# FFN first products turned round: the activations stand still, 512 weight columns move, and the gated values are turned back by TensorE

## The reference

```python
def rms_norm(x, g):
    y = xf * lax.rsqrt(jnp.mean(xf * xf, axis=-1, keepdims=True) + EPS)
    return (y * g.astype(jnp.float32)).astype(x.dtype)

def swiglu(h, w_gu, w_down):          # w_gu: 1024 x 5632, w_down: 2816 x 1024
    gate, up = jnp.split(h @ w_gu, 2, axis=-1)
    return (jax.nn.silu(gate) * up) @ w_down

x = x + 0.5 * swiglu(rms_norm(x, norm_ffn1[i]), w_ffn1_gu[i], w_ffn1_down[i])
```

## Time and profile before

| what | us |
|---|---|
| three runs | 1745.28, 1748.50, 1748.54 (median 1748.5) |
| the profiled execution: own time | 1747.14 |
| its span in the trace | 1745.4 |
| TensorE busy | 1680.4 (96%) |
| VectorE busy | 1073.2 (61%) |
| ScalarE busy | 797.5 (46%) |
| GpSimd busy | 158.6 (9%) |

### The profile page before, as it was taken

The page is one execution under the profiler, slowest core; times in us unless marked ns, Lnnn a source line. Parts: engine busy times, 40 slices in busy tenths (PEclk is TensorE's granted clock), DMA queues, the critical chain, the costliest instruction groups (busy, mean ns, idle before and its releaser), DMA issues.

```text
span 1745.4 us, 29133 instructions
## 1 busy us (share of the span) xinstructions
PE 1680.4 (96%) x12214; PEld 1579.1 (90%) x12214; DVE 1073.2 (61%) x1043; ACT 797.5 (46%) x934; POOL 158.6 (9%) x121
## 2 busy tenths in 40 slices
PE   7999998899999999999999999888999999999998
PEld 7999986799999999999999998776899989888997
DVE  6555776376456765678464686665665567556563
ACT  5443458254335543456343553544544465444442
POOL 1000122010001100012000135111000001100000
PEclk9999999999999999999999999888999999999999
DMA  7545451155454545454544353203255535325551
GB/s 278 216 150 213 151 185 75 73 200 186 174 194 164 198 165 197 172 200 184 187 182 178 146 204 145 97 25 120 79 211 177 184 145 193 108 110 187 178 189 48
DMA packets 39631, 282.26 MB, mean 162 GB/s; under 512 B 4416, under 2 KB 4544, under 8 KB 5760
## 3 DMA queue, kind: packets, MB, share of 16 engines
q1 hardware_dynamic: 39168, 279.59, 43.2%
q0 software_dynamic: 384, 1.51, 0.2%
HBM read 280.04 MB, written 1.05 MB: 161 GB/s over the span
## 4 chain that ended last, share of the span: by engine, by line
PE 88%; DVE 5%; ACT 4%; DMA 1%; issue 1%; POOL 1%; POOLq 0%; DVEq 0%; SPq 0%; ACTq 0%
PE ps L318 27%; PE ps L321 27%; PE ps L322 27%; DVE w_lo L1352 1%; DMA raw<-weights 1%; ACT arena L1166 1%; ACT w_hi L988 1%; PE ps L640 1%; PE ps L419 1%; PE ps L684 1%; DMA arena<-nsa_tables 0%; POOL arena L2015 0%; DVE arena L1647 0%; ACT arena L1018 0%; DVE arena L1588 0%
## 5 line engine op out<-in xcount | busy, mean ns | idle before, releaser
L318 PE MATMUL ps<-hT_hi,w_hi 128*128 128x256 f32 x2392 | 682.9, 285 | 14.2 <-DVE hT_lo L1364 11.3
L1352 DVE TENSOR_TENSOR w_lo<-raw,w_hi 128x2048 fp32r<-128x2048 f32 x264 | 600.8, 2299 | 139.0 <-ACT w_hi L988 139.0
L321 PE MATMUL ps<-hT_lo,w_hi 128*128 128x256 f32 x2392 | 678.7, 284 | 0.0
L322 PE MATMUL ps<-hT_hi,w_lo 128*128 128x256 f32 x2392 | 678.7, 284 | 0.0
L988 ACT ACTIVATE w_hi<-raw 128x2048 fp32r<-128x2048 f32 x264 | 495.2, 1903 | 56.3 <-DMA raw<-weights 50.7
L318 PEld LDWEIGHTS ps<-hT_hi,w_hi 128*128 128x128 f32 x2392 | 460.9, 193 | 17.3 <-DVE w_lo L1352 11.3
L321 PEld LDWEIGHTS ps<-hT_lo,w_hi 128*128 128x128 f32 x2392 | 461.2, 193 | 1.9 <-issue 0.7
L322 PEld LDWEIGHTS ps<-hT_hi,w_lo 128*128 128x128 f32 x2392 | 460.8, 193 | 0.0
L321 PE MATMUL ps<-hid_lo,w_hi 128*128 128x256 f32 x744 | 211.3, 284 | 0.0
L318 PE MATMUL ps<-hid_hi,w_hi 128*128 128x256 f32 x744 | 210.6, 283 | 0.0
L322 PE MATMUL ps<-hid_hi,w_lo 128*128 128x256 f32 x744 | 208.3, 280 | 0.0
(11 more groups left out here) (260 smaller groups left out, 1749.7 us busy)
## 6 DMA issues: line engine op xcount, KB each, us to landing
raw<-weights SPq DMA_DIRECT2D x264, 1024.0 KB, 4.8
X<-x SPq DMA_DIRECT2D x2, 512.0 KB, 7.3
out<-X SPq DMA_DIRECT2D x4, 256.0 KB, 2.1
arena<-p POOLq DMA_DIRECT2D x2, 256.0 KB, 5.4
arena<-counts POOLq DMA_DIRECT2D x1, 512.0 KB, 5.3
arena<-nsa_tables POOLq DMA_DIRECT2D x1, 448.0 KB, 7.3
const<-constants SPq DMA_DIRECT2D x1, 427.0 KB, 9.9
cols<-parameters SPq DMA_DIRECT2D x1, 213.5 KB, 2.7
```

The costliest lines, as they stand in the source:

```text
L318: mm = nc.tensor.matmul(dst, a_hi, b_hi, start=start, stop=False, skip_group_check=True)
L321: nc.tensor.matmul(dst, a_hi, b_lo, start=False, stop=False, skip_group_check=True)
L322: return nc.tensor.matmul(dst, a_lo, b_hi, start=False, stop=stop, skip_group_check=True)
L1352: nc.vector.tensor_tensor(unit_cols(w_lo, u, 0, UNIT), raw[:, r * UNIT:(r + 1) * UNIT], f(unit_cols(w_hi, u, 0, UNIT)), ALU.subtract).then ...
```

## The change

In FFN stages alone, `up` becomes `up_rows`: a 128 x 128 tile of `hT` (128 tokens) is stationary, and 512 weight columns (256 gate, 256 up) move, 2 token tiles x 3 products x 8 chunks, 48 matmuls of 512 columns. A bank then holds 128 tokens on the partitions, with gate and up side by side. ScalarE takes the silu straight from PSUM with `rstd` as the scale of each partition, in two halves of 256 columns; VectorE multiplies up by `rstd` and by that silu in one instruction for each half. `spread` goes from FFN stages. The product now has tokens on the partitions, and `down` wants hidden values there, so TensorE turns it with 4 transposes of 128 x 128 (`turn`) into the bank that the gates have left; `hid_hi` and `hid_lo` read that bank.

`turn(0)` stands ahead of chunk 4 of `up_rows(1)`, `turn(j)` for j from 1 to 9 ahead of chunk 1 of `up_rows(j + 1)`, and `turn(10)` ahead of the last quarter of `down(9)`.

```diff
@@ TensorE
-            def down(u, h, first, last, t=None):
+            def down(u, h, first, last, t=None, mid={}):
...
                 for b in range(4):
+                    if b in mid:
+                        mid[b]()
...
+                def up_rows(us, b0, fresh, t, mid):
+
+                    for k in range(KC):
+                        if k in mid:
+                            mid[k]()
+                        u, a = us[k // 4], k % 4 * 512
+                        if k % 4 == 0:
+                            unit_ready(u, t)
+                        if fresh:
+                            pe.wait_ge(*hT_ready.due(me))
+                        for tok in range(TT):
+                            mm = three(bank(b0 + tok), lhs(hT_hi, k, tok), lhs(hT_lo, k, tok), unit_cols(w_hi, u, a, 512), unit_cols(w_lo, u, a, 512),
+                                       k == 0, k == KC - 1)
+                            if (k, tok) == (KC - 1, 0):
+                                mm.then_inc(gu_full.sem, 1)
+                        if k % 4 == 3:
+                            mm.then_inc(unit_used.sem, 1)
+
+                def turn(j, t=None):
+
+                    pe.wait_ge(*rows_ready.due(me, turn=t))
+                    for c in range(HC):
+                        for tok in range(TT):
+                            mm = nc.tensor.transpose(bank(2 * (j % 2), c * TOKENS + tok * P, P), at(ACT_AT + tok * 256 + c * P, P), ident)
+                    mm.then_inc(rows_turned.sem, 1)
+
...
-                one(1, u0 + 2, mid={2: lambda: spread(7)})
+                rstd_ready.due(me)
+                one(1, u0 + 2, mid={4: lambda: turn(0)})
...
-                        one(2 + b, u + 3 * b, t)
+                        one(2 + b, u + 3 * b, t, {1: lambda: turn(1 + b, t)})
...
-                one(FFN_BLOCKS - 1, u)
+                one(FFN_BLOCKS - 1, u, mid={1: lambda: turn(FFN_BLOCKS - 2)}, in_down={3: lambda: turn(FFN_BLOCKS - 1)})
@@ ScalarE
-                    act.wait_ge(*scaled.due(me, turn=t))
-                    nc.scalar.activation(sil[:, 0:512], sil[:, 0:512], ACT.Silu).then_inc(silu_done.sem, 1)
+                    act.wait_ge(*gu_full.due(me, turn=t))
+                    nc.scalar.activation(sil[:, 0:256], bank(b0, 0, 256), ACT.Silu, scale=rstd[:, 0:1]).then_inc(silu_done.sem, 1)
+                    act.wait_ge(unit_used.sem, u + 2 + more)
+                    nc.scalar.activation(sil[:, 256:512], bank(b0 + 1, 0, 256), ACT.Silu, scale=rstd[:, 1:2]).then_inc(silu_done.sem, 1)
...
-                    act.wait_ge(*hid_ready.due(me, turn=t))
-                    if j and not last:
-                        act.wait_ge(unit_used.sem, u + 3 + more)
-                    nc.scalar.activation(chunk(hid_hi, HC if last else 0, HC), at(ACT_AT, 512), ACT.Copy).then_inc(hid_hi_done.sem, 1)
+                    act.wait_ge(*rows_turned.due(me, turn=t))
+                    nc.scalar.activation(chunk(hid_hi, HC if last else 0, HC), bank(b0), ACT.Copy).then_inc(hid_hi_done.sem, 1)
@@ VectorE
-                    times_rstd(sil[:, 0:512], bank(b0)).then_inc(scaled.sem, 1)
-                    times_rstd(second, bank(b0 + 1)).then_inc(second_scaled.sem, 1)
-                    nc.vector.tensor_tensor(at(ACT_AT, 512), sil[:, 0:512], second, ALU.mult).then_inc(hid_ready.sem, 1)
+                    for tok in range(TT):
+                        dve.wait_ge(*silu_done.due(me, turn=t))
+                        ins = nc.vector.scalar_tensor_tensor(at(ACT_AT + tok * 256, 256), bank(b0 + tok, 256, 256), rstd[:, tok:tok + 1],
+                                                             sil[:, tok * 256:(tok + 1) * 256], ALU.mult, ALU.mult)
+                    ins.then_inc(rows_ready.sem, 1)
...
-                    nc.vector.tensor_tensor(chunk(hid_lo, h, HC), at(ACT_AT, 512), f(chunk(hid_hi, h, HC)), ALU.subtract).then_inc(hid_split.sem, 1)
+                    nc.vector.tensor_tensor(chunk(hid_lo, h, HC), bank(b0), f(chunk(hid_hi, h, HC)), ALU.subtract).then_inc(hid_split.sem, 1)
```

More of the change, by code:

```diff
@@ L248, in network_kernel @@
         gu_full, scaled, silu_done, second_scaled = S("gu_full"), S("scaled"), S("silu_done"), S("second_scaled")
+        rows_ready, rows_turned = S("rows_ready"), S("rows_turned")
         hid_ready, hid_hi_done, hid_split = S("hid_ready"), S("hid_hi_done"), S("hid_split")
@@ L473, in ffn @@
             def ffn(s, u0):
-                def one(j, u, t=None, mid={}):
-                    up([u, u + 1], 2 * (j % 2), 4, gu_full, j == 0, t, mid)
+                def up_rows(us, b0, fresh, t, mid):
[14 more added lines that the diff above has]
+                            mm.then_inc(unit_used.sem, 1)
@@ new lines, in turn, with one @@
+                def turn(j, t=None):
[4 more added lines that the diff above has]
+                    mm.then_inc(rows_turned.sem, 1)
+                def one(j, u, t=None, mid={}, in_down={}):
+                    up_rows([u, u + 1], 2 * (j % 2), j == 0, t, mid)
@@ L478, in one @@
                     if j:
-                        down(u + 2, 0, j == 1, False, t)
+                        down(u + 2, 0, j == 1, False, t, in_down)
                 one(0, u0, mid={6: lambda: sums(s)})
-                one(1, u0 + 2, mid={2: lambda: spread(7)})
+                rstd_ready.due(me)
+                one(1, u0 + 2, mid={4: lambda: turn(0)})
                 u = u0 + 5
                 with pe.Fori(0, 4) as i:
-                    t = Turn(i, {hid_split: 2}, 6)
+                    t = Turn(i, {hid_split: 2, rows_ready: 2}, 6)
@@ L957, in ple @@
                 pe.wait_ge(*p_ready.due(me))
-                pe.wait_ge(rstd_read.sem, norm_of[s] + 1 - sum(kind in ("stick", "pool") for kind, _ in stages[:s]))
+                pe.wait_ge(rstd_read.sem, norm_of[s] + 1 - sum(kind in ("stick", "pool", "ffn") for kind, _ in stages[:s]))
                 for m in range(KC):
@@ L1023, in ffn @@
             def ffn(s, u0):
+                act.wait_ge(rstd_ready.sem, norm_of[s] + 1)
                 def one(j, u, t=None):
                     more = t.i * t.units if t else 0
[L1028 to L1029 removed]
+                    b0 = 2 * (j % 2)
+                    act.wait_ge(*gu_full.due(me, turn=t))
+                    nc.scalar.activation(sil[:, 0:256], bank(b0, 0, 256), ACT.Silu, scale=rstd[:, 0:1]).then_inc(silu_done.sem, 1)
+                    act.wait_ge(unit_used.sem, u + 2 + more)
+                    nc.scalar.activation(sil[:, 256:512], bank(b0 + 1, 0, 256), ACT.Silu, scale=rstd[:, 1:2]).then_inc(silu_done.sem, 1)
                     last = j == FFN_BLOCKS - 1
@@ L1043, in ffn @@
                 with act.Fori(0, 4) as i:
-                    t = Turn(i, {scaled: 2, hid_ready: 2}, 6)
+                    t = Turn(i, {gu_full: 2, rows_turned: 2}, 6)
                     for b in range(2):
                         one(2 + b, u + 3 * b, t)
-                scaled.due(me, 2 * 3)
-                hid_ready.due(me, 2 * 3)
+                gu_full.due(me, 2 * 3)
+                rows_turned.due(me, 2 * 3)
                 split[me] += 3 * 6
@@ L1307, in ple @@
             def ple(s, u0):
+                gu_full.due(me, 2)
                 nc.scalar.preload_act_table(ACT.Sigmoid)
@@ L1422, in ffn @@
                 split_to(u0 + 5)
-                take_rstd(7)
+                dve.wait_ge(rstd_ready.sem, norm_of[s] + 1)
                 one(0, u0)
@@ L1426, in ffn @@
                 u = u0 + 5
-                each = {silu_done: 2, second_scaled: 2, hid_hi_done: 2, hid_split: 2, gu_full: 2}
+                each = {silu_done: 4, hid_hi_done: 2}
                 with dve.Fori(0, 4) as i:
@@ L1436, in ffn @@
                 one(FFN_BLOCKS - 1, u)
-                hid_split.due(me)
+                gu_full.due(me, FFN_BLOCKS)
+                hid_split.due(me, FFN_BLOCKS)
             def mlp(s, u0):
```

8 lines of the change are left out of this document (1 added, 7 removed).

## The result

The changed kernel takes 1755.03 us (median of 10 runs, 1751.28 to 1757.21), the kernel before 1745.43 us (10 runs, 1743.79 to 1748.99). The ratio is 1.0049, with a 95% interval of 1.0040 to 1.0058: slower by half a per cent. The profiled execution took 1752.62 us, its span is 1750.9 us.

What follows compares the result with a forecast made beforehand. TensorE's list and its waits at stage ends were taken as the bound: -10.0 on the list, +6.9 at stage starts, +7.7 at ends, +4.6 us in all, forecast 1753.0 us (slower by little), range 1744 to 1760.

Steps and rivals of the forecast that it cites:

- First products: FFN blocks: 48 matmuls of 512 columns replace 96, 11.52 us becoming 10.89 a block; term -27.7 us.
- Rival 6: First products: both shapes cost the same for each column, 0.240 us, so nothing is gained; 1780.8 us, chance 0.02.
- list gain of 10.0 us: TensorE's list alone: -27.7 for first products, +19.5 for the turns, -1.8 for spread, or -10.0 us.
- Transposes: Four transposes of each block's turn cost 0.443 us, +19.5 us over 44 blocks; bounds +10 and +26.
- Rivals 1: A turn hides behind the products, four transposes costing perhaps 0.23 us; faster, 1743.7 us, chance 0.08.
- 5 (0.53 to 0.6): A turn costs 0.53 to 0.6 us, for fixed costs at both ends; 1757 to 1760 us, chance 0.10.
- Steady blocks: Middle of a stage: VectorE's idle 6.04 us covers the later silus, products and splits; costed at nothing.
- `turn(0)`: Start of an FFN stage: TensorE waits for the sixth unit's split, 2.5, 1.1, 3.0 and 0 us; +6.9 us.
- Rival 3: Start of a stage: turn(0) is covered, since the sixth unit's transfer comes earlier; 1746.2 us, no difference, chance 0.12.
- `turn(10)`: End of a stage: late hid_hi delays down(10) by 0.13 us and the next stage by 1.5 or 2.1; +7.7 us.
- Rival 2: End of a stage: block 10's late hid_hi costs nothing, the two splits not being held; 1745.4 us, chance 0.12.
- Rival 4: TensorE's clock falls after the 2.5 and 3.0 us waits, one or two falls; 1754.8 to 1756.5 us, chance 0.17.

Runs made afterwards that it cites:

- after_again: The changed kernel profiled once more with nothing edited; this execution took 1753.79 us.
- turn10_early: The changed kernel with turn(10) ahead of the second quarter of down(9) instead of the last; 1743.44 us, ratio 0.9981 to the kernel before.
- turns_doubled: The changed kernel with every transpose of a turn issued twice, to the same place; 1769.43 us, ratio 1.0142.
- the shifted kernels: The kernel before with 15 or 27 surplus matmuls in the last PLE stage, so NSA begins later; 1750.37 and 1751.83 us, ratios 1.0020 and 1.0022.
- both_moved: The changed kernel with turn(10) ahead of down(9)'s second quarter and turn(0) ahead of chunk 6 of up_rows(1); 1739.02 us, ratio 0.9954 to the kernel before.
- turn0_late: The changed kernel with turn(0) ahead of chunk 6 of up_rows(1) instead of chunk 4; 1748.78 us, ratio 1.0013 to the kernel before.

## Why the prediction was right, and where it was off

The forecast was 1753.0 us, the measured median 1755.0; slower by little was the likeliest case, and in the FFN stages it came by the mechanism that was named. That the time came within 2 us of the forecast is partly luck, as the sum at the end shows. Point by point:

**First products.** Forecast 10.89 us a block; measured 10.96. The gain is 0.56 us a block instead of 0.634. Rival 6, at 0.240 us for 512 columns, is excluded. The rule of the Trainium skill that was weighed there ("TensorE: Matmul & The Clock Gate", section "Back-to-back issue gap") would leave 0.12 us (not 0.13), 5.3 us in all: the trace goes against it here, at 0.227 us for 512 columns and 0.117 to 0.120 for 256, where it gives 0.216 and 0.109. The same section of the Trainium skill calls that rule the gap of an isolated matmul and gives about 131 ns at N = 512 for a stream of weight loads and matmuls, which the prediction left out; the trace does not bear that figure out either.

**`down`.** It was costed at no change, and is a term that the sum lacked. Its 48 matmuls take 5.62 us for 5.76, with unchanged shapes. The steady block is 17.02 us (16.99 in the second and fourth stage) instead of the forecast 17.09, a further 3 us over 44 blocks. The forecast's list gain of 10.0 us holds some 1.9 us of the first six chunks of `up(0)`, which lie ahead of the stretches above; inside them it was 8.1, and 11.05 was measured.

**Transposes.** 0.443 us was taken for a `turn`, 0.44 is in the changed kernel's rows, and 0.39 to 0.41 was the cost of four more. Rivals 1 (0.23) and 5 (0.53 to 0.6) are excluded.

**Steady blocks.** No `turn(j)` from 1 to 9 waits, as forecast: VectorE's idle time was cover enough.

**`turn(0)`.** Forecast 2.5, 1.1, 3.0 and 0 us; idle time 0.97, 0.95, 2.56 and 0, and by starts, as the forecast counted, 1.13, 1.11, 2.72 and 0. The first was the bad one. It rested on the split at 30.30, 7.58 us behind `sums`; in the three other executions of the kernel before the same split stands at 27.84, 27.98 and 28.02, 5.8 to 6.2 us behind its `sums`, and in the changed kernel at 27.59, 6.46 behind. So a row of one execution's first microseconds, where transfers set the pace, was read as the kernel's. The idle time ahead of this `turn(0)` stays the least certain: 0.97, 0.70 and 0.17 us in the changed kernel, after_again and turn10_early. Rival 3, that the wait is covered, is true of the fourth stage only.

**`turn(10)`.** Forecast 1.5, 2.1, 1.5 and 2.1 us ahead of the next stages; idle time 1.42, 2.01, 1.42 and 2.01, and by starts 1.57, 2.17, 1.57 and 2.16. Ahead of `down(10)` 0.13 us in each stage was forecast; by starts it is 0.23, since TensorE gets there 0.1 us earlier with 36 products of `down(9)` at 0.117 us. Rival 2 is excluded, by these rows and by turn10_early.

**The clock.** Rival 4 came in three of the four profiled executions that had the long wait of the third stage: in the changed kernel, in after_again and in turn10_early. TensorE's timeline of the changed kernel just behind it, and the stretches around:

```profile
588.09 0.42 PE L319 MATMUL ps<-w_hi,hT_hi 128*128 128x512 f32 x1
588.33 0.61 PE L322 MATMUL ps<-w_lo,hT_hi 128*128 128x512 f32 x1
```

```profile
583.00:586.00 3.00, 1.34 (x6) 0.76 (x5) 0.04 (x2) 2.40 (x3) 0.00 (x0) 1.00 1.03 396
586.00:592.00 6.00, 5.09 (x18) 4.11 (x19) 4.62 (x5) 4.43 (x4) 0.00 (x0) 0.72 0.36 145
592.00:595.00 3.00, 3.00 (x17) 2.53 (x16) 3.00 (x2) 0.78 (x2) 0.00 (x0) 1.00 0.86 311
```

The engine had waited 2.56 us, was at full speed for 1.4 us again, and then the products lasted 0.61 us instead of 0.39. A mean of 0.72 over 6 us is 3.4 us at 1.2 GHz, which do the work of 1.7. The dense products behind the transposes, which the forecast held against this rival, did not prevent it; its chance of 0.17 was too low. Its size was right. The argument against it also misread: in the kernel before there is no second wait there, and the clock was at 1.00 up to 1416.9 and at 0.50 from 1417, in the midst of the transposes behind the one wait of 2.76 us. But the fall does not follow from the wait alone. turns_doubled, with the same wait and eight transposes behind it, had none; TensorE's timeline and the stretch behind it:

```profile
597.89 1.09 PE L502 MATMUL ps<-const,arena 128*128 128x128 f32 x8 [2.46 <-DVE arena L1438]
```

```profile
598.00:604.00 6.00, 6.00 (x31) 5.13 (x32) 4.35 (x3) 4.41 (x4) 0.00 (x0) 1.00 0.27 98
```

**Sum.** In the FFN stages the forecast was +4.6 for the whole, of which +6.5 inside the stretches; measured is +4.0 and +5.1. Against the 6.5, the +4.0 is made up of a list that is 3.0 us shorter, waits of 13.4 us by starts instead of 14.6, and 1.7 us lost to the clock. That the median still came out at +9.6 goes, by the runs sorted by clock, with a thing that the prediction did not have at all: the granted clock in parts that the change does not touch. It was also made against a median of three runs of 1748.5, which ten runs put at 1745.4; the two errors partly cancel, which is the luck in the number. What remains open is why the changed kernel never had an execution at 0.983: its own falls explain 1.7 us of it (3.4 in after_again, which had a second one), the shifted kernels don't settle the rest.

## What to carry to other kernels

Price a reordering in two sums, the list of the engine that is the bound and every wait that a moved instruction brings: here 11 us were gained on the list of the FFN stages and 15 lost, and placing two groups of four transposes elsewhere gave those 15 back (of the 11, the whole kernel shows 8.0, with 4.9 to 11.2 as its interval). Count a wait from start to start: the idle time of the profile was 0.16 us too little for each one here. A transpose that stands in an in-order stream belongs where its input has been ready for some time and where nothing waits for its output; at the head and the tail of a stage both have to be read anew, since the place that is safe in a steady block is not safe there. When two kernels are half a per cent apart, compare the stretches that the edit touches in two profiled executions of each, and the clock of the timed runs, before the median is explained by the edit.

## What the hardware showed that was not expected

- 256-column products behind 512-column ones go at 0.117 us each (48 in 5.62 us), where the same products among their like went at 0.120. Transposes undo it: in both_moved the first 12 products of `down(9)` are 0.117 us apart and the 84 behind `turn(10)` 0.120; in the changed kernel those of `down(10)`, with no 512-column product ahead but the wait of 0.23 us, are 0.117 apart again. No run tells why.
- The clock fell at waits of 2.43 to 2.56 us in three of four profiled executions (2.43, 2.51 and 2.56 with a fall, 2.46 without; in turn10_early the clock is already low in the transposes right behind the wait). Of the eight waits of 1.87 to 2.02 us at the ends of stages, three had a fall behind them (1.87 us in turns_doubled, 2.02 in turn0_late and after_again) and five had none (2.01 three times, 1.88 twice). So the length of the wait alone does not decide it. The stretches of turn0_late behind its wait of 2.02 us show 0.74 and 0.69, where the changed kernel with a wait of 2.01 us at the same place shows 1.00:

```profile
536.00:539.00 3.00, 2.44 (x15) 2.47 (x16) 3.00 (x7) 3.00 (x8) 0.71 (x1) 0.74 0.95 382
539.00:542.00 3.00, 3.00 (x20) 3.00 (x20) 3.00 (x3) 3.00 (x5) 2.84 (x3) 0.69 0.01 5
```

```profile
535.00:541.00 6.00, 3.99 (x34) 3.82 (x33) 6.00 (x11) 4.91 (x12) 1.92 (x2) 1.00 0.79 311
541.00:547.00 6.00, 6.00 (x52) 6.00 (x52) 3.72 (x5) 5.37 (x4) 3.04 (x4) 1.00 0.01 1
```

- One stage with sparse TensorE work, the NSA part, took from 215.7 to 223.4 us in four executions of one and the same kernel.
